# The second layer of a two-layer decoder step: sample queries projected first, the first attention scores ahead of the last query turn, and selection rounds moved ahead of the attention loop

## The reference, cut to what matters

```python
def odd_mixer(h, past_k, past_v, past_kidx, w_in, w_out):
    proj = jnp.einsum('ntd,de->nte', h, w_in)
    q, k, v, qi, ki, wi = jnp.split(proj, [s1, s2, s3, s4, s5], axis=-1)
    q = rope(q.reshape(n, t, H_C, HEAD_DIM), pos_q)        # 16 heads of 64
    k = rope(k.reshape(n, t, KV_C, HEAD_DIM), pos_q)       # 4 heads
    qi = rope(qi.reshape(n, t, H_IDX, D_IDX), pos_q)       # 8 index heads
    ki = rope(ki[:, :, None, :], pos_q)[:, :, 0]
    ...
    o = dsa_attention(q, k_all, v_all, qi, ki_all, wi * (H_IDX ** -0.5), pos_q, pos_k)
    return jnp.einsum('nte,ed->ntd', o.reshape(n, t, H_C * HEAD_DIM), w_out), k, v, ki

def dsa_attention(...):                                    # for each block of queries
    dots = jnp.einsum('nqhe,nke->nqhk', qi_blk, k_idx) * idx_scale
    score = jnp.einsum('nqhk,nqh->nqk', jax.nn.relu(dots), wi_blk)
    score = jnp.where((pos_k[None, :] <= pq_blk[:, None])[None], score, -jnp.inf)
    _, sel = lax.top_k(score, n_sel)
    s = jnp.einsum('nqgrd,nqkgd->nqgrk', qg, k_sel) * scale
    p = jax.nn.softmax(jnp.where(valid, s, -jnp.inf), axis=-1)
    o = jnp.einsum('nqgrk,nqkgd->nqgrd', p, v_sel)
```

## Time and profile before

| | |
|---|---|
| median of 3 runs | 1524.99 us (1523.49 to 1525.87) |
| the profiled execution | 1524.35 us, its span 1522.6 us |
| PE busy | 1347.2 us, 88% of the span |
| DVE busy | 575.6 us, 38% |
| ACT busy | 304.9 us, 20% |
| POOL busy | 185.6 us, 12% |
| PE's share of the chain that ended last | 23% (DMA 7%, DVE 6%) |
| pages of a sample | 8 issues of 256 KB, median 3.0 us from issue to landing |

### The profile page before, as it was taken

How to read it: one execution, slowest core, us unless ns; L and a number is a source line. 1 busy time by engine, 2 the same in 40 slices (tenths; PEclk the granted TensorE clock), 3 DMA queues, 4 the chain that set the end, 5 groups by cost and what they waited for, 6 DMA issues and landing times. The chain is left out here.

```text
span 1522.6 us, 28236 instructions
## 1 busy us (share of the span) xinstructions
PE 1347.2 (88%) x10889; PEld 760.9 (50%) x10890; DVE 575.6 (38%) x1420; ACT 304.9 (20%) x777; POOL 185.6 (12%) x469
## 2 busy tenths in 40 slices
PE   7999998899789989999499997888998799988990
PEld 3444454454555546555443444555646465555650
DVE  2169842252513111111547993665314322111115
ACT  2121143321100000001313114455501000000002
POOL 1010190001010000000201662000000100000002
PEclk9999999899889999999699999899998799999996
DMA  8523577774558999999401132333434479999975
GB/s 271 200 56 112 176 227 232 225 270 144 180 182 327 362 394 368 396 408 384 148 5 56 32 111 82 102 96 108 156 126 144 173 291 364 391 384 392 396 290 198
DMA packets 87385, 341.04 MB, mean 224 GB/s; under 512 B 25671, under 2 KB 32935, under 8 KB 73286
## 3 DMA queue, kind: packets, MB, share of 16 engines
q1 hardware_dynamic: 67246, 289.40, 51.9%
q0 software_dynamic: 10656, 37.56, 7.2%
q10 hardware_dynamic: 9344, 12.20, 2.3%
HBM read 309.00 MB, written 30.47 MB: 223 GB/s over the span
## 5 line engine op out<-in xcount | busy, mean ns | idle before, releaser
L1213 PE MATMUL banks<-arena 128*32 128x128 f32 (+1 forms) x4736 | 362.5, 336 | 24.2 <-DMA arena<-in_wstream 14.2
L1213 PEld LDWEIGHTS banks<-arena 128*32 128x32 f32 (+1 forms) x4736 | 242.0, 127 | 144.0 <-issue 50.3
L1241 PE MATMUL banks<-arena 128*64 128x512 f32 (+1 forms) x1184 | 173.5, 492 | 1.1 <-ACT arena L1693 1.1
L1798 DVE TENSOR_TENSOR arena<-arena,banks 128x256 f32<-128x256 f32 (+5 forms) x84 | 38.5, 459 | 278.6 <-PE banks L1213 182.8
L892 PE MATMUL banks<-arena 128*128 128x512 f32 x320 | 141.8, 597 | 0.5 <-DMA arena<-in_wstream 0.4
L2167 DVE COPY arena<-banks 128x256 f32<-128x256 f32 (+1 forms) x56 | 21.4, 382 | 291.9 <-PE banks L1226 285.6
L1798 DVE TENSOR_TENSOR arena<-banks,arena 128x512 f32<-128x512 f32 (+5 forms) x159 | 70.7, 474 | 134.9 <-ACT arena L1617 85.8
L1119 PE MATMUL banks<-arena 128*128 128x512 f32 x256 | 113.9, 602 | 3.6 <-ACT arena L1733 2.3
L920 PE MATMUL banks<-arena 128*128 128x512 f32 x256 | 116.4, 599 | 0.0
L1693 ACT ACTIVATE arena<-banks 128x512 f32<-128x512 f32 (+1 forms) x56 | 29.6, 529 | 372.1 <-PE banks L1241 372.1
L1241 PEld LDWEIGHTS banks<-arena 128*64 128x64 f32 (+1 forms) x1184 | 59.0, 123 | 84.2 <-issue 69.8
(11 more groups left out here) (282 smaller groups left out, 1459.3 us busy)
## 6 DMA issues: line engine op xcount, KB each, us to landing
arena<-in_wstream SPq DMA_DIRECT2D x109, 2048.0 KB, 13.3
arena<-in_fox_kt SPq DMA_DIRECT2D x64, 256.0 KB, 3.0
arena<-in_fox_v SPq DMA_DIRECT2D x64, 256.0 KB, 3.0
arena<-in_dsa_page SPq DMA_DIRECT2D x64, 256.0 KB, 3.0
expert_rows<-arena ACTq DMA_DIRECT2D x76, 128.0 KB, 9.0
expert_rows<-arena POOLq DMA_DIRECT2D x1, 6656.0 KB, 19.4
hn_scratch<-arena POOLq DMA_DIRECT2D x8, 512.0 KB, 3.0
expert_rows<-arena ACTq DMA_DIRECT2D x68, 32.0 KB, 8.3
```

Of the source, the lines that this page charges most:

```text
L1213: last = mm(bank(b, 0, 4 * n, n * j, n * j + n), x[:, c, :], w[:, c, 4 * n * j:4 * n * j + 4 * n], start=(c == 0), stop=(c == DC - 1))
L1241: last = mm(bank(3, 0, 8 * n, n * q, n * q + n), ht2[g % 2][:, 128 * i + n * j:128 * i + n * j + n], w[:, c, 8 * n * q:8 * n * q + 8 * n], ...
L1798: return v.tensor_tensor(out, x, y, op)
```

## The change

Three things change, all in layer 1.

1. The query jobs 10 to 14 and 15 to 19 take the tiles in the order 4, 0, 1, 2, 3, as the index queries did. Copies, rotary and turns follow (`odd_job`, `odd_query`). `qbd_half(1)` now waits for `turn_ev1` 13 instead of 17, `qbd_half(0)` for 18 instead of 22.
2. PE issues scores(0) and `score_s(0, 0)` ahead of the last turn, which is now part of `late` together with the wait for `turn_ev1` 22; ahead of scores(0) it waits for `turn_ev1` 20 and `proj_ev1` 20. ACT issues the exponentials of job 0 ahead of the last turn's copy.
3. DVE does 2 rounds of tile 2 between the two `qbd_half`, and 6 behind the second. In the loop, tile 2's last 8 rounds are one each in iterations 0 to 7, and tile 3's 16 rounds in iterations 8 to 22 (before: 12 rounds in iterations 0 to 9, and 16 in 10 to 22).

```diff
+    FRONT_TILES = (4, 0, 1, 2, 3)
+    def odd_job(job):
+        return 3 - job // 5, job % 5 if 5 <= job < 10 else FRONT_TILES[job % 5]
+    def odd_query(n):
+        return 1 - n // 5, FRONT_TILES[n % 5]
...
             scores(0)
+            if l == 1:
+                score_s(0, 0)
+                late()
             for i in range(jobs + 1):
...
                 elif d == 0:
                     first(i)
-                    if s == 0:
-                        score_s(0, 0)
...
+        def late():
+            beside(87)
+            pe.wait_ge(S("turn_ev1"), upto("turn_ev1", 22))
+
         project_odd(beside)
         beside(83)
-        beside(87)
-        pe.wait_ge(S("turn_ev1"), upto("turn_ev1", 22))
+        pe.wait_ge(S("turn_ev1"), upto("turn_ev1", 20))
+        pe.wait_ge(S("proj_ev1"), upto("proj_ev1", 20))
...
             exps(0)
+            if l == 1:
+                late()
...
-        beside(87)
-        attend(1, 0, 8)
+        attend(1, 0, 8, lambda: beside(87))
...
         def qbd_half(b):
-            dve.wait_ge(S("turn_ev1"), upto("turn_ev1", 17 if b else 22))
+            dve.wait_ge(S("turn_ev1"), upto("turn_ev1", 13 if b else 18))
...
         select_prompt(2, 0, 2)
-        select_prompt(2, 2, 4)
         qbd_half(0).then_inc(S("qbd1"), 1)
+        select_prompt(2, 2, 8)
 
         def beside(i):
-            if i < 10:
-                select_prompt(2, 4 + 6 * i // 5, 4 + 6 * (i + 1) // 5)
+            if i < 8:
+                select_prompt(2, 8 + i, 9 + i)
             elif i < 23:
-                select_prompt(3, 16 * (i - 10) // 13, 16 * (i - 9) // 13)
+                select_prompt(3, 16 * (i - 8) // 15, 16 * (i - 7) // 15)
```

More of the change, by code:

```diff
@@ L414, in ride @@
         return jobs, where, sample
-    INDEX_TILES = (4, 0, 1, 2, 3)
+    FRONT_TILES = (4, 0, 1, 2, 3)
[3 more added lines that the diff above has]
+        return 1 - n // 5, FRONT_TILES[n % 5]
     block = ctx.enter_context(nc.Block())
@@ L739, in rope_q @@
         def rope_q(n):
-            t, b = n % 5, 1 - n // 5
+            b, t = odd_query(n)
             pool.wait_ge(S("proj_ev1"), upto("proj_ev1", 10 + n + 1))
@@ L910, in project_odd @@
             for job in range(20):
-                b, (t, c0, c1) = 3 - job // 5, TILES[INDEX_TILES[job] if job < 5 else job % 5]
+                b, (t, c0, c1) = odd_job(job)[0], TILES[odd_job(job)[1]]
                 k = first_block(1, "in") + b
@@ L936, in turn, with attend @@
             last.then_inc(S(f"turned{l}"), 1)
-        def attend(l, q, k, v, qb, keys, new_k, bias, vals, chunks, strip):
+        def attend(l, q, k, v, qb, keys, new_k, bias, vals, chunks, strip, late=None):
             jobs, where, sample = ride(l)
@@ L1422, in beside @@
                 x = (h - 3) // 2
-                t = INDEX_TILES[x]
+                t = FRONT_TILES[x]
                 pe.wait_ge(S("i_roped"), x + 4)
@@ L1474, in _ @@
                              sels[64 * min(i, 1):64 * min(i, 1) + 64, (0, 0, 512)[i]:(512, 512, 520)[i]]),
-               lambda s, kt: g3(kv_odd[s % 2], NPG)[:, kt, 256:512], 2, 64)
+               lambda s, kt: g3(kv_odd[s % 2], NPG)[:, kt, 256:512], 2, 64, late)
         out_project(1)
@@ L1574, in project_odd @@
             for job in range(20):
-                b, t = 3 - job // 5, INDEX_TILES[job] if job < 5 else job % 5
+                b, t = odd_job(job)
                 dst, sc = ((A0[:, t, 0:512], 0.125), (A0[:, t, 512:1024], 0.125), (A3[:, t, :], 1.0),
@@ L1587, in project_odd, with attend @@
                 beside(4 * job + 3)
-        def attend(l, chunk0, nch):
+        def attend(l, chunk0, nch, late=None):
             jobs, where, sample = ride(l)
@@ L1758, in beside @@
                 x = (h - 3) // 2
-                turned(2 + x, qi[:, :, cols(INDEX_TILES[x])])
+                turned(2 + x, qi[:, :, cols(FRONT_TILES[x])])
             if 16 <= at < 28:
```

## The result

| | before | after |
|---|---|---|
| median | 1524.24 us (6 runs) | 1513.64 us (6 runs) |
| profiled execution, its span | 1524.35, 1522.6 us | 1515.22, 1513.5 us |

The ratio after to before is 0.9935, with a 95% interval of 0.9907 to 0.9963. The prediction was 1514.0, faster. Three later executions, two of the changed kernel and one of e5, took 4242 to 6750 us and are left out of every ratio and median here; no trace of them was kept.

What follows compares the result with a forecast made beforehand. It saw attention bound by a serial chain POOL, PE, ACT, PE and by second rounds in loop iterations. Front 4.6, loop 4.6 and clock 1.5 summed to 10.7 us, giving 1514.0 us, range 1508.5 to 1519.5.

Steps and rivals of the forecast that it cites:

- The front: From the last projection job to scores(2): work placed under the last rotary gains 4.6 us, 3.5 to 5.1.
- The rounds: Attention loop: fewer iterations with two selection rounds on DVE gain 4.6 us, bounds 2 and 5.9.
- Iteration 7: Loop: the comparison and scaling that close tile 2 move here, where PE already waited 0.25; a loss of 0.96 us.
- The room that was left for the pages: Sample 2's pages landed about 3.5 us ahead of their scores; a microsecond of the gain may stay behind there.
- The upper bound of 5.9: Top of the loop's round gain, in us, if iteration 7's closing pair is covered.
- The clock: Attention: shorter waits leave PE less time at the low clock; +1.5 us, with -3 and +4.5 as ends.
- two low stretches: Loop, behind waits at 953.94 and 1024.39: if both went, 1.6 us at iteration 18, up to 2.9 at iteration 6.
- Behind attention: After attention nothing is tied to an earlier time, so the gain is carried to the end as a shift.
- Half a gain: Rival: low clock stays at the loop's start, pages or ACT take over iterations 4 and 9's waits; 5.5 us, chance 0.23.
- The large gain: Rival: both low stretches go and the start runs at full speed; about 14.5 us, 1510, chance 0.11.
- Slower: Rival: many short waits keep the clock low; with 30 us of further low clock in the loop 1530, chance 0.03.
- The experts eat it: Rival: the experts, at their weight loads, absorb attention's gain; time within 3 us of before, chance 0.05.

Runs made afterwards that it cites:

- e5: e4 with POOL issuing four of the eight page loads of samples 2 to 7; median 1489.94 us, ratio to the kernel before 0.9781.
- e3: The changed kernel with the last query turn again ahead of scores(0) and score_s(0, 0); ratio to the kernel before 0.9984.
- e2: The kernel before with only the selection rounds spread as in the changed kernel, 8 of tile 2 ahead of the loop; ratio 0.9976.
- e1: The changed kernel with the selection rounds spread as before, so only the front changes; median 1521.42 us, ratio to the kernel before 0.9979.
- e4: The changed kernel with DVE's rounds moved to where it stood idle, 10 of tile 2 ahead of the loop; ratio to the kernel before 0.9841.
- e6: e5 with the last query tile's rotary moved from POOL to DVE; median 1493.11 us, ratio to the kernel before 0.9792.

## Why the prediction was right

**The front.** Forecast 4.6 (3.5 to 5.1), measured 5.1. Its steps held one by one, each counted from the projection's end: the copy of the projection, the rotary of 4.2 us unchanged, a wait of under 1.5 us as good as met (1.54), DVE there in time, with 2.7 us to spare instead of the 1.4 at least. e3 shows that the work placed under the rotary is the gain, as the forecast had it. In its old place that work took 4.9 us, 1.57 from scores(0) to scores(1) and 3.35 for the sample scores, at a clock that was low for most of it; the prediction calls all of the 3.35 half clock, but the last of it already ran faster (1.57 us for L1000, against 1.97 in e2). e1 shows the lower bound: with the same waits and a fallen clock the gain is 3.6.

**The rounds.** Forecast 4.6. The marks of the two timelines, each counted from scores(2), give the terms. Iteration 4: scores(7) at 19.44 before and 18.19 after, 1.25 as forecast. Iteration 7: `turn_o` waits 0.99 more, forecast 0.96. Iteration 8: PE's wait grew from 1.11 to 1.38, so 0.3 is lost, as forecast. Iteration 9: from the masking wait of iteration 8 to `value_s(2)` 1.98, forecast 1.7. Iteration 14: the wait is 1.1 shorter, forecast 1.4. Iteration 18: 1.5, as forecast. That adds up to 4.6. One small loss was not foreseen: 0.3 in iterations 15 and 16, with a new wait of 0.18 for masking. The room that was left for the pages was not needed: they landed in time here, and only e4, which runs faster, waits for them. The upper bound of 5.9 is wrong as a sum: 4.6 and the covered 0.96 make 5.6. That has no weight here.

**The clock.** Forecast 1.5 (-3 to 4.5). The loop gained 7.4 in all, so 3.1 remain beside the round terms and the small loss. Of the two low stretches that the prediction named, one stayed: behind the wait of 1.07 us at 950.07 the clock was low again, and a little longer than before, so iteration 6 lost 0.3. The other, at iteration 18, went: `value_s` took 2.33 instead of 3.67, and the stretch won 1.6, as forecast. A third, in iterations 12 and 13, went as well, for 0.4. These three make 1.8, against the 1.5 forecast. The last 1.3 came in iteration 22, where both kernels wait the same 3.03 us; since the second profile of the kernel before has as much of it without any change, it can't be credited to the change. Against that profile the loop's whole gain is 5.8 to 5.9. The trace bears out the Trainium skill ("TensorE: Matmul & The Clock Gate", "A second HAM failure mode: psum-queue depth-cycling") in that short idle times between groups of matmuls make the clock swing (a wait of 1.07 us was followed by 7 us at a mean of 0.55); but its consequence in the prediction, that low stretches would only move and the term be 0, did not hold. With half of the idle time gone (e4) the loop's mean is 0.99, and with another 4 us gone (e5) it is 1.00.

**Behind attention.** The rest took 423.2 to 427.4 us in all ten profiles, with no order in it. This agrees with a gain that is carried to the end, but the spread is two fifths of the gain, so it can't show that nothing is lost there. It is also why the forecast's 10.7 and the measured 10.6 agree better than their parts: 12.5 in attention by the first pair of profiles, less what chance took elsewhere. That the numbers meet to 0.1 us is luck. The second set of executions has the changed kernel at 1516.84 against 1525.22, 8.4 us faster, at the lower end of the forecast's 8 to 13.5.

**The rivals.** "Half a gain", 5.5 us, can't be excluded by the time of the second set alone (4.0 to 10.5 us by its interval), but its mechanism is not what the profiles show: neither pages nor ACT took over the waits of iterations 4 and 9. The large gain would have needed the low clock of iteration 6 to go as well. "Slower" would have needed a low clock in more of the loop; none of the kernels showed that. (Its threshold of 21 us of low clock doesn't follow from its own half microsecond for each: 9.2 us need 18.) "The experts eat it" gets no support from the column of the rest: 424.2 and 425.6 before, 425.1 and 423.9 after.

**What the prediction missed** lay beside its steps: it priced the second rounds and took one round in each iteration as given. What was left, mostly single rounds, cost more than what went: moving them, and two of them out of the loop, gained another 15.1 us (e4), three times the 4.6 forecast for the rounds of the change.

## What to carry to other kernels

Background work that an in-order engine does between two steps of a loop belongs right behind the step that others wait for, and ahead of a step that would wait anyway; look for idle time of the engine just before the step that follows (e4, which also spread the work differently). When PE hands work round with other engines in a ring, a wait costs more than its idle time, since PE is also busy for longer behind it at half clock: from the kernel before to e5 the loop's idle time fell by 17.0 us and its busy time, for the same work, by 11.4. A reorder that puts independent work under a fixed chain gains about the time that this work took in its old place, low clock and all (4.9 of the 5.1 us here), though under the chain it takes only 2.4. Moving a link of the chain to a faster engine gained nothing here (e6), where that engine has the next link too. And read a small gain in more than one profile: two of the same kernel differed by 1.5 us in the loop, a fifth of what was to be explained.

## What the hardware showed that was not expected

- The same idle times don't always let the clock fall. Behind waits of 1.54 to 1.56 and then 0.69 us PE kept 2.4 GHz in the changed kernel (both profiles), e4 and e5, and fell to 1.2 GHz in e1. In the changed kernel's loop a wait of 1.07 us was followed by 7 us at a mean of 0.55, three of 1.38 to 1.43 us (at 989.5, 1009.5 and 1030.1) by none, and one of 1.38 at 970.4 by 3.5 us at a mean of 0.53. Behind the wait of 3.03 or 3.04 us in iteration 22 `value_s` took 4.30 and 3.02 us in two profiles of the kernel before, 3.79 and 3.73 in two of the changed one, and 2.33, full speed, in e2 and e3.
- A page load held the issuing queue for about a microsecond on both engines that issued it: 8.0 us for eight on SP (922.02 to 930.02, before), about 1.14 us each on POOL (e5). On both queues at once (e5) the waits of 4.6 us for pages were gone, although each page took longer from issue to landing: a median of 4.4 us on SP's queue and 4.8 on POOL's, against 2.9 in e4.
- DVE does the rotary's six instructions of 128x256 in 2.23 us (e6), POOL in 4.2.
